# First attention of a fused two-block transformer kernel: the product of probabilities and values as three rounded products, two steps behind the scores

## The reference, cut to what matters

```python
def block(qblk):
    s = jnp.einsum('bqhgd,bkhd->bhgqk', qblk, k, preferred_element_type=jnp.float32) * scale
    p = jax.nn.softmax(s, axis=-1).astype(v.dtype)
    return jnp.einsum('bhgqk,bkhd->bqhd', p, v)

o = lax.map(block, qb)
o = jnp.moveaxis(o, 0, 1).reshape(B, S, N_HEADS * HEAD_DIM)
return o @ w_o
```

## Time and profile before

| what | value |
|---|---|
| median of 3 runs | 1960.36 us (1959.1 to 1962.41) |
| profiled execution, its own time | 1958.75 us |
| profiled execution, span from first to last instruction | 1957.0 us |
| mean granted TensorE clock | 0.999 of full |
| PE / PEld / DVE / ACT / POOL busy | 99% / 82% / 56% / 38% / 30% of the span |

### The profile page before, as it was taken

How to read it: one execution, slowest core, us unless ns; L and a number is a source line. 1 busy time by engine, 2 the same in 40 slices (tenths; PEclk the granted TensorE clock), 3 DMA queues, 4 the chain that set the end, 5 groups by cost and what they waited for, 6 DMA issues and landing times.

```text
span 1957.0 us, 23604 instructions
## 1 busy us (share of the span) xinstructions
PE 1935.6 (99%) x9254; PEld 1599.5 (82%) x9254; DVE 1096.7 (56%) x1086; ACT 751.1 (38%) x838; POOL 590.4 (30%) x528
## 2 busy tenths in 40 slices
PE   9999999999999999999999999999999999999998
PEld 7766888888887988888888887889888888888886
DVE  6854455565466547454555467874353474545455
ACT  6556332322244435332322245355553253222223
POOL 1201389996000002389995001523300100000000
PEclk9999999999999999999999999999999999999999
DMA  6411244343323220244443323413133312322221
GB/s 227 112 12 31 88 184 161 140 166 108 107 75 111 91 102 22 81 178 166 140 166 102 107 86 114 119 44 87 44 108 108 108 65 67 106 88 104 88 105 65
DMA packets 42764, 204.51 MB, mean 105 GB/s; under 512 B 13249, under 2 KB 13377, under 8 KB 20161
## 3 DMA queue, kind: packets, MB, share of 16 engines
q1 hardware_dynamic: 34784, 167.82, 25.3%
q0 software_dynamic: 7904, 35.66, 6.0%
HBM read 190.84 MB, written 2.10 MB: 99 GB/s over the span
## 4 chain that ended last, share of the span: by engine, by line
PE 93%; DVE 3%; ACT 1%; issue 1%; DMA 1%; POOL 0%; SPq 0%; POOLq 0%; DVEq 0%; ACTq 0%
PE ps L261 24%; PE ps L263 24%; PE ps L262 24%; PE ps L694 3%; PE ps L2546 2%; PE ps L2545 2%; PE ps L2547 2%; PE ps L1757 1%; PE ps L293 1%; PE ps L291 1%; PE ps L292 1%; PE ps L661 1%; PE ps L681 1%; PE ps L680 1%; PE ps L1741 1%
## 5 line engine op out<-in xcount | busy, mean ns | idle before, releaser
L223 ACT ACTIVATE w_hi<-w_raw 128x2048 fp32r<-128x2048 f32 x141 | 270.3, 1917 | 713.4 <-PE ps L263 642.0
L231 DVE TENSOR_TENSOR w_lo<-w_raw,w_hi 128x2048 fp32r<-128x2048 f32 x139 | 323.1, 2324 | 112.2 <-ACT w_hi L223 110.2
L261 PE MATMUL ps<-h_hi,w_hi 128*128 128x512 f32 (+1 forms) x968 | 380.5, 393 | 4.0 <-DVE w_lo L231 2.9
L263 PE MATMUL ps<-h_hi,w_lo 128*128 128x512 f32 (+1 forms) x968 | 370.8, 383 | 0.0
L262 PE MATMUL ps<-h_lo,w_hi 128*128 128x512 f32 (+1 forms) x968 | 370.5, 383 | 0.0
L1529 POOL TENSOR_SCALAR ada_t<-ada_w,prm 128x256 f32<-128x256 f32 x192 | 220.2, 1147 | 13.3 <-DMA ada_w<-in_ada 12.4
L261 PEld LDWEIGHTS ps<-h_hi,w_hi 128*128 128x128 f32 x968 | 182.2, 188 | 42.2 <-issue 6.3
L263 PEld LDWEIGHTS ps<-h_hi,w_lo 128*128 128x128 f32 x968 | 182.0, 188 | 35.9
L262 PEld LDWEIGHTS ps<-h_lo,w_hi 128*128 128x128 f32 x968 | 182.3, 188 | 34.7 <-issue 1.7
L1051 DVE TENSOR_TENSOR x<-x,ps 128x1024 f32<-128x1024 f32 x128 | 155.7, 1216 | 79.8 <-PE ps L263 79.8
L261 PE MATMUL ps<-m_xhi,w_hi 128*128 128x512 f32 x512 | 200.2, 391 | 0.0
(11 more groups left out here) (360 smaller groups left out, 3069.7 us busy)
## 6 DMA issues: line engine op xcount, KB each, us to landing
w_raw<-in_wb SPq DMA_DIRECT2D x152, 1024.0 KB, 4.9
ada_w<-in_ada POOLq DMA_DIRECT2D x24, 1024.0 KB, 5.3
a_sw<-a_g POOLq DMA_DIRECT2D x20, 128.0 KB, 2.7
x<-in_xT SPq DMA_DIRECT2D x4, 512.0 KB, 7.8
ada_w<-ada_acc POOLq DMA_DIRECT2D x4, 384.0 KB, 5.2
out<-f_pad SPq DMA_DIRECT2D x3, 512.0 KB, 2.6
w_raw<-in_wb SPq DMA_DIRECT2D x4, 256.0 KB, 6.2
w_hi<-a_q POOLq DMA_DIRECT2D x4, 256.0 KB, 3.7
```

The lines of the kernel that those rows point to most:

```text
L223: act.activation(w_hi[:, slot], w_raw[:, slot], ACT.Copy).then_inc(hi_done, 1)
L231: dve.tensor_tensor(w_lo[:, slot], w_raw[:, slot], w_hi[:, slot].bitcast(F32), ALU.subtract).then_inc(split_done, 1)
L261: pe.matmul(out, w[0], h[0], start=start, stop=False)
L263: return pe.matmul(out, w[1], h[0], start=False, stop=stop)
```

## The change

The values are split into `a_vh` (ScalarE) and `a_vl` (VectorE), and the exponentials into `p_hi` and `p_lo`. ScalarE's Exp now writes a float32 buffer (`sq`, two slots), a second ScalarE instruction rounds it to `p_hi`, and VectorE subtracts to get `p_lo`. `values(s)` becomes two calls of `three`, six float32r matmuls, and is issued two steps behind `scores`. Some of ScalarE's and VectorE's work between the steps moves by a step, and the low part of the output tiles moves from GpSimd to VectorE.

```diff
         h_at = ExitStack()
-        a_p = sb("a_p", [P, 4, 1024], F32, h_at)
+        p_hi = sb("p_hi", [P, 4, 2 * S], F32R, h_at)
+        p_lo = sb("p_lo", [P, 4, 2 * S], F32R, h_at)
...
-        STEPS, HEADS, LEAD, A_LAG = 32, 16, 4, 1
+        STEPS, HEADS, LEAD, A_LAG = 32, 16, 4, 2
+        probs_hi = lambda s: 9 + s + (2 if s >= 1 else 0)
+        probs_lo = lambda s: 5 + s + (1 if s >= 3 else 0)
+        queries_hi = lambda a, r: 2 * a + r + (1 if a < V_BLOCK - 1 else 2)
+        ready_for = lambda a: a + 1 if a < V_BLOCK - 1 else probs_lo(2) + 1
...
                 if p % 8 == 0:
-                    pe.wait_ge(a_ready, p // 8 + 2)
+                    pe.wait_ge(a_ready, ready_for(p // 8 + 1))
...
-                pe.wait_ge(a_exp, s + 1)
+                pe.wait_ge(a_ready, probs_lo(s))
                 for i in range(2):
-                    k = 2 * (s % 2) + i
-                    last = pe.matmul(ps[:, h % 2, :], at_["a_v"][:, k, kv_of(h), :], a_p[:, s % 4, i * S:(i + 1) * S], start=k == 0, stop=k == TT - 1)
+                    k, w = 2 * (s % 2) + i, slice(i * S, (i + 1) * S)
+                    last = three(pe, ps[:, h % 2, :], (at_["a_vh"][:, k, kv_of(h), :], at_["a_vl"][:, k, kv_of(h), :]),
+                                 (p_hi[:, s % 4, w], p_lo[:, s % 4, w]), k == 0, k == TT - 1)
                 last.then_inc(a_PV, 1)
...
+            values(STEPS - 2)
             project(range(2))
             values(STEPS - 1)
...
             def probs(s):
                 act.wait_ge(a_S, s + 1)
+                if s >= 2:
+                    act.wait_ge(a_ready, probs_lo(s - 2))
+                pair = 3 - s % 2
+                act.activation(two(sq[:, s % 2]), pair_(pair), ACT.Exp).then_inc(a_exp, 1)
+                act.wait_ge(a_exp, s + 1)
                 if s >= 4:
                     act.wait_ge(a_PV, s - 3)
-                pair = 3 - s % 2
-                act.activation(two(a_p[:, s % 4]), pair_(pair), ACT.Exp).then_inc(a_exp, 1)
+                act.activation(p_hi[:, s % 4], sq[:, s % 2], ACT.Copy).then_inc(a_qhi, 1)
...
                 if s == 0:
                     take_v(1)
-                if s == 1:
                     q_hi(V_BLOCK - 1)
-                if s >= 3 and s % 2 == 1 and (s - 3) // 2 < HEADS:
-                    inverse((s - 3) // 2)
-                if s >= 6 and s % 4 == 2 and (s - 6) // 4 < KT:
-                    out_hi((s - 6) // 4)
+                if s >= 4 and s % 2 == 0 and (s - 4) // 2 < HEADS:
+                    inverse((s - 4) // 2)
+                if s >= 7 and s % 4 == 3 and (s - 7) // 4 < KT:
+                    out_hi((s - 7) // 4)
...
+            def v_low(i):
+                dve.wait_ge(a_v_in, i + 1)
+                dve.wait_ge(a_vset, 3)
+                for t in (2 * i, 2 * i + 1):
+                    for r in range(2):
+                        dve.scalar_tensor_tensor(out=v_heads("a_vl", r)[:, t], in0=v_tokens(r)[:, t], scalar=V_ROOT[:, t:t + 1],
+                                                 in1=v_heads("a_vh", r)[:, t].bitcast(F32), op0=ALU.mult, op1=ALU.subtract)
+
+            def low_probs(s):
+                dve.wait_ge(a_qhi, probs_hi(s))
+                if s >= 4:
+                    dve.wait_ge(a_PV, s - 3)
+                dve.tensor_tensor(p_lo[:, s % 4], sq[:, s % 2], p_hi[:, s % 4].bitcast(F32), ALU.subtract).then_inc(a_ready, 1)
+
+            def out_low(t):
+                dve.wait_ge(a_oh, t + 1)
+                dve.tensor_tensor(a_q2[:, t, 1, :], at_["a_o"][:, t % 2, :], a_q2[:, t, 0, :].bitcast(F32), ALU.subtract).then_inc(a_ol, 1)
...
-            for s in range(STEPS + 4):
+            for s in range(STEPS + 6):
                 if s + LEAD < STEPS:
                     top(s + LEAD)
-                if s in (2, 4):
-                    low(V_BLOCK - 1, s // 2 - 1)
-                if s >= 4 and s % 2 == 0 and (s - 4) // 2 < HEADS:
-                    normed((s - 4) // 2)
+                if s < 2:
+                    v_low(s)
+                if s >= 5 and s % 2 == 1 and (s - 5) // 2 < HEADS:
+                    normed((s - 5) // 2)
+                if s < STEPS:
+                    low_probs(s)
+                if s == 2:
+                    for r in range(2):
+                        low(V_BLOCK - 1, r)
+                if s >= 8 and s % 4 == 0 and (s - 8) // 4 < KT:
+                    out_low((s - 8) // 4)
...
         def attn_pool(pool):
-            pool.memset(at_["a_v"][:], 1.0).then_inc(a_vset, 1)
+            pool.memset(at_["a_vh"][:].bitcast(F32), 1.0).then_inc(a_vset, 1)
...
+            pool.wait_ge(a_rows, V_BLOCK)
+            pool.wait_ge(a_vset, 2)
+            pool.memset(at_["a_vl"][:].bitcast(F32), 0.0).then_inc(a_vset, 1)
             pool.wait_ge(a_S, 1)
             queries(3)
             queries(4)
-            for t in range(KT):
-                pool.wait_ge(a_oh, t + 1)
-                pool.tensor_tensor(a_q2[:, t, 1, :], at_["a_o"][:, t % 2, :], a_q2[:, t, 0, :].bitcast(F32), ALU.subtract).then_inc(a_ol, 1)
```

More of the change, by code:

```diff
@@ L99, in build @@
             at_ = {n: sb(n, s, d, scope) for n, s, d in [
-                ("a_kh", [P, 4, S], F32R), ("a_kl", [P, 4, S], F32R), ("a_v", [P, TT, 4, P], F32), ("a_nmax", [P, 64], F32R)]}
+                ("a_kh", [P, 4, S], F32R), ("a_kl", [P, 4, S], F32R), ("a_vh", [P, TT, 4, P], F32R), ("a_nmax", [P, 64], F32R)]}
             with ExitStack() as s2:
@@ L105, in build @@
             with ExitStack() as s2:
+                at_["a_vl"] = sb("a_vl", [P, TT, 4, P], F32R, s2)
                 at_.update({n: sb(n, s, F32, s2) for n, s in [
-                    ("a_pad0", [P, 2, 1024]), ("a_o", [P, 2, S]), ("a_pad1", [P, 1024]), ("a_inv", [P, S])]})
+                    ("a_o", [P, 2, S]), ("a_pad1", [P, 1024]), ("a_inv", [P, S])]})
             sb("a_pad2", [P, 9, 1024], F32, scope)
@@ L767, in take_v @@
                     for r in range(2):
-                        ins = act.activation(v_heads("a_v", r)[:, t], v_tokens(r)[:, t], ACT.Copy, scale=V_ROOT[:, t:t + 1])
+                        ins = act.activation(v_heads("a_vh", r)[:, t], v_tokens(r)[:, t], ACT.Copy, scale=V_ROOT[:, t:t + 1])
                 ins.then_inc(a_v_in, 1)
@@ L853, in low @@
                     dve.wait_ge(a_rows, a + 1)
-                dve.wait_ge(a_qhi, 2 * a + r + 1)
+                dve.wait_ge(a_qhi, queries_hi(a, r))
                 rot = two(at_["a_rot"][own[r], a % 2])
@@ L927, in queries @@
                 for r in range(2):
-                    pool.wait_ge(a_qhi, 2 * a + r + 1)
+                    pool.wait_ge(a_qhi, queries_hi(a, r))
                     to = half[0:64, (a - 1) // 2].rearrange("p (t r s) -> p t r s", t=2, r=2)[:, :, r, :]
```

## The result

The kernel after takes 1970.43 us (median of 5 runs, 1969.59 to 1970.9), the kernel before 1959.68 us beside it (5 runs, 1957.96 to 1962.41): a ratio of 1.0055, 95% interval 1.0044 to 1.0067. The profiled execution took 1969.59 us at a mean granted clock of 0.997, with a span of 1967.9, 10.9 longer than before.

What follows compares the result with a forecast made beforehand. The prediction took TensorE, busy 99% of the span, to bound the kernel before. Its terms, 5.3 + 4.1 + 2.5 - 0.2 + 1.5 = +13.2 us on 1960.4, gave 1973.6, rounded to 1973.5, range 1966 to 1980.

Steps and rivals of the forecast that it cites:

- The ring: Attention steps: Exp, Copy, low_probs, top and next maxima close a chain, 6.30 us for two steps, 13.25 for four.
- The expected signs: Profile after: maxima every 3.25 to 3.35 us, TensorE waiting for top on nearly every step, top right behind low_probs.
- The start: Attention iterations 0 to 4: iteration 4 begins at 107.7 where it was 102.37, +5.3 us.
- Steps 4 to 27 and the quarters: Attention iterations 4 to 27: longer steps +4.1 us, weight-block quarters on VectorE and ScalarE together +2.5 us.
- The tail: From iteration 27 through steps 28 to 31 to the eighth projection tile: -0.2 and +1.5 us.
- Work against order (first rival): Attention steps: sums of engine work, not order, set the step; -4 to -6 us, about 1955.5; chance 7%.
- The clock (third rival): Start of attention: TensorE idles before iterations 3 and 4, its clock falls; +3 to +6 us, 1976 to 1980; chance 10%.
- The short chain (second rival): Attention steps: chain holds at 3.17 us a step, start absorbed, quarters free; +6 us or down to no change; chance 12%.

Runs made afterwards that it cites:

- late_low: Kernel after with VectorE issuing low_probs one step later, behind the next top, and the last queries' low part moved from step 2 to 3: 1960.86 us, ratio 1.0009.
- the two pads: Kernel after plus twelve unused 256-column VectorE additions in even steps 4 to 26, ahead of low_probs (1971.17 us) or right behind it (1974.60 us).
- pad_before: Kernel after plus one unused 256-column VectorE addition ahead of low_probs in each even step 4 to 26: 1971.17 us, ratio 1.0061.
- best: Kernel after with low_probs a step later, second v_low and last queries' low parts later, VectorE's weight-block quarters at steps 28 to 31: 1960.17 us, ratio 1.0005.
- pool_out: Kernel after with the low part of the output tiles made on GpSimd again, not on VectorE: 1972.03 us, ratio 1.0062.
- warm: Kernel after with ten small float32 matmuls of ones in TensorE's idle time before iteration 2: 1970.81 us, ratio 1.0058.
- lag_clean: Kernel after with values one step behind scores, and inverse, out_hi, normed and out_low at the steps that fit this lag: 1973.12 us, ratio 1.0066.
- lag_one: Kernel after with values one step behind scores instead of two, nothing else moved to fit: 2013.87 us, ratio 1.028.

## Why the prediction was right, step by step

Forecast were 1973.5 us and +13.2 over the kernel before; measured are 1970.43 and +10.75. The profiles differ by 10.9, of which the early iteration 0 takes off 0.7 that no step of the forecast foresaw.

**The ring.** It holds, and its size too: 6.33 us for two steps against 6.30, 13.14 and 13.13 for four steps (iterations 12 to 16 to 20) against 13.25. `late_low` opens it with one moved call and gets 9.6 of the 10.7 us back, about a third of it at the start; the two pads show that in iterations 12 to 20 a delay costs its full price inside it and nothing outside. The expected signs are there: VectorE's `top` right behind `low_probs`, ScalarE waiting 17.8 us for scores where it waited 41.1. TensorE waits for `top` in 9 of the 13 iterations from 108 to 150 us, by 0.4 us on average, and not on nearly every one. From iteration 4 to 20 single ones take 2.90 to 3.55 us; only their mean, 3.25 (3.28 from iteration 12 to 20), is in the range of 3.25 to 3.35.

**The start.** +5.2 against +5.3. One idle stretch was missed, the 2.55 us before iteration 2. The slower matmuls behind it filled the 2.5 us that the prediction had before iteration 3; the one before iteration 4 came, with 1.57 against 1.9. `low_probs(0)` began at 94.43 and `top(5)` at 95.57 in the profile that is 0.7 early, as worked out. Iteration 4 stood at 106.85, with the same 0.7 counted at 107.6, against 107.7. The small `v_low` took 1.12 for four, against 1.13 from ScalarE's row.

**Steps 4 to 27 and the quarters.** Together +5.7 against +6.6, the larger of the two mis-sized terms. The steps I had 0.03 us each too long: iterations 4 to 20 took 51.93 and not 52.45 (0.1 of it is my sum, in which 2 x 6.30 stands as 12.7; iterations 4 to 8 took 12.60). Iterations 20 to 27 took 25.37 where 23.2 + 2.5 = 25.7 was forecast, and of this miss 0.2 is again the step, so the quarters together were right to 0.1. How they divide between VectorE and ScalarE no run shows.

**The tail.** +0.8 against +1.3. The Exp of step 28 began at 188.40, 4.25 after iteration 27 and not 4.4; from there to the eighth tile it was 21.96, against 22.0. The same way in the kernel before is 20.79, not the 20.5 of my sum.

**Work against order (first rival).** Refuted for this kernel. In the windows row from 106 to 186 us no engine is busy more than 89% of 80 us (TensorE 71.17, VectorE 69.33, ScalarE 67.56), and yet a step can't be shorter. The Trainium skill's page "Perfetto Trace Analysis" (Identifying the Most-Contended Engine) takes the engine with the highest occupancy as the bottleneck, but judges TensorE by its weight loads, since its pipelined matmuls make the busy time a poor measure. Its weight loads are 51.89 of 80 us, so by that rule VectorE would have been worked on. Yet pad_before gives VectorE more work and iterations 12 to 20 stay as long; what counts is where in its stream the work stands. In `late_low` and `best` the rule comes nearer, with an engine at 41.13 of 42 and 34.16 of 35, though in `late_low` that is VectorE while the chain that ended last names ScalarE (39.72).

**The clock (third rival).** Its mechanism came true beside the forecast, and the price I gave it (+3 to +6) was wrong: I had put the slower matmuls on the chain, and in iteration 2 they ran while VectorE's work took as long. Where it falls again in iteration 4, as in both pads and pool_out, that iteration is about 1.5 us longer, of which 0.8 is left at iteration 12 in pad_before.

**The short chain (second rival).** Each link came out within 0.06 us of the rows it was taken from, so neither the short nor the long end was reached. That the sum is right to 0.03 is partly luck: `low_probs` until `top` was 1.14 and not 1.20, `top` until `maxima` 1.34 and not 1.28.

What stays open: why the clock falls once at the start in one execution and twice in others, why it falls between 1180 and 1192 us in the profiles of warm, pool_out and lag_clean and not in the kernel after, and why iteration 0 comes up to 0.7 us earlier in some profiles. By itself a difference of 1 to 2 us between two of these profiles is therefore no evidence of an edit's effect.

## What to carry to other kernels

When an instruction that waits for a late engine is put into an in-order stream, look at what stands behind it, and follow that to the engine that started the chain. If it closes a ring, the step is the length of the ring divided by the steps that it spans, and busy shares don't show it. Put the late instruction behind the one that the bottleneck waits for: one moved call was worth 9.6 us here. And a gain in one engine's work counts only down to the next engine's sum, 2.87 us a step here and not 2.80, with everything that was hidden in idle time (quarters, the last steps) now at its price.

## What the runs showed of the hardware

- TensorE's granted clock fell to 0.53 over 6.8 us (96.2 to 103) after a single idle stretch of 2.55 us in the kernel after; behind a stretch of the same 2.55 us in pool_out it was 0.75 over the same window. Idle stretches of 2.8 us on average (30.6 us in 11 waits, one at every second step) went with 0.82 on average over 100 us. How much of lag_one's 43 us the clock is, no run shows.
- A GpSimd subtraction of 512 columns and a VectorE subtraction of 512 columns that overlap stretched VectorE's from 0.68 to 1.78 us, once. In six other places of pool_out GpSimd's started while `low_probs` ran, and there GpSimd's took 1.79 to 1.82 us, against 1.29 with VectorE idle, and `low_probs` stayed at 1.22 to 1.23. GpSimd's multiplication by a constant of the same size, 1.50 us, left VectorE's subtractions at 1.20 to 1.23.
- ScalarE's rounding Copy of 1024 columns costs 1.058 us on average, the Exp of the same size from PSUM 1.024.
